# Conditioning chunks of a two-block transformer kernel: from TensorE to VectorE and GpSimd in the first stream

## What is computed

```python
c_act = jax.nn.silu(c)
mod = c_act @ w_ada[l] + b_ada[l]              # (1, 2048) @ (2048, 12288)
sh1, sc1, g1, sh2, sc2, g2 = jnp.split(mod[:, None, :], 6, axis=-1)
```

## Time and profile before

| | |
|---|---|
| median of 3 runs | 3177.53 us (3170.0 to 3181.22) |
| the profiled execution | 3168.41 us, its span 3166.3 us |
| first stream | from the start to about 428 us of the span |
| busy over the span | PE 3005.4 us (95%), PEld 77%, DVE 2092.3 us (66%), ACT 48%, POOL 279.8 us (9%) |
| mean granted clock of TensorE | 0.978 of full speed |
| DMA | 737.98 MB, mean 233 GB/s |

### The profile page before, as it was taken

How to read it: one execution, slowest core, us unless ns; L and a number is a source line. 1 busy time by engine, 2 the same in 40 slices (tenths; PEclk the granted TensorE clock), 3 DMA queues, 4 the chain that set the end, 5 groups by cost and what they waited for, 6 DMA issues and landing times. The chain is left out here.

```text
span 3166.3 us, 43444 instructions
## 1 busy us (share of the span) xinstructions
PE 3005.4 (95%) x17552; PEld 2439.7 (77%) x17552; DVE 2092.3 (66%) x2363; ACT 1510.1 (48%) x1829; POOL 279.8 (9%) x134
## 2 busy tenths in 40 slices
PE   7999978998899999998999999999996999999997
PEld 7888956966776678776788878878785888888886
DVE  5557647365899967766458868745666566666666
ACT  4345522243777755554344475555444444444443
POOL 0000002000000000000000000000003433443330
PEclk9999978999999999998999999999998999999999
DMA  7988567088999978772666744664765566666663
GB/s 263 339 271 298 173 232 290 12 315 306 325 378 348 378 251 271 268 250 82 211 225 218 234 151 158 216 225 160 272 213 186 199 212 213 209 215 212 213 205 125
DMA packets 358136, 737.98 MB, mean 233 GB/s; under 512 B 19957, under 2 KB 118370, under 8 KB 344527
## 3 DMA queue, kind: packets, MB, share of 16 engines
q1 hardware_dynamic: 342740, 710.58, 65.4%
q10 hardware_dynamic: 15228, 25.05, 2.2%
HBM read 708.93 MB, written 26.65 MB: 232 GB/s over the span
## 5 line engine op out<-in xcount | busy, mean ns | idle before, releaser
L288 DVE TENSOR_TENSOR moe_w_lo<-ring,moe_w_hi 128x1024 fp32r<-128x1024 f32 x384 | 458.0, 1222 | 132.7 <-ACT moe_w_hi L278 127.9
L288 DVE TENSOR_TENSOR mx_w_lo<-ring,mx_w_hi 128x1024 fp32r<-128x1024 f32 (+1 forms) x288 | 346.8, 1210 | 279.0 <-ACT mx_w_hi L278 275.3
L278 ACT CAST moe_w_hi<-ring 128x1024 fp32r<-128x1024 f32 x384 | 395.6, 1049 | 247.1 <-PE psum L304 242.6
L278 ACT CAST mx_w_hi<-ring 128x1024 fp32r<-128x1024 f32 (+1 forms) x288 | 296.7, 1036 | 421.2 <-PE psum L304 400.4
L288 DVE TENSOR_TENSOR mlp_w_lo<-ring,mlp_w_hi 128x1024 fp32r<-128x1024 f32 x256 | 318.1, 1244 | 264.5 <-ACT mlp_w_hi L278 263.6
L278 ACT CAST mlp_w_hi<-ring 128x1024 fp32r<-128x1024 f32 x256 | 268.1, 1050 | 407.8 <-PE psum L304 399.1
L304 PE MATMUL psum<-mx_w_hi,mx_a_hi 128*128 128x496 f32 (+1 forms) x1024 | 405.8, 396 | 5.5 <-DVE mx_w_lo L288 4.1
L304 PE MATMUL psum<-mx_w_lo,mx_a_hi 128*128 128x496 f32 (+1 forms) x1024 | 397.7, 388 | 0.0
L304 PE MATMUL psum<-mx_w_hi,mx_a_lo 128*128 128x496 f32 (+1 forms) x1024 | 397.6, 388 | 0.0
L288 DVE TENSOR_TENSOR in_w_lo<-ring,in_w_hi 128x628 fp32r<-128x628 f32 x192 | 155.2, 813 | 167.3 <-ACT in_w_hi L278 165.3
L304 PE MATMUL psum<-in_w_hi,in_a_hi 128*128 128x314 f32 x768 | 242.7, 316 | 2.5 <-DVE in_a_lo L251 1.4
(11 more groups left out here) (615 smaller groups left out, 5728.5 us busy)
## 6 DMA issues: line engine op xcount, KB each, us to landing
ring<-in_w_ada SPq DMA_DIRECT2D x80, 1024.0 KB, 9.2
ring<-in_w_e_gate SPq DMA_DIRECT2D x64, 1024.0 KB, 6.6
ring<-in_w_e_up SPq DMA_DIRECT2D x64, 1024.0 KB, 7.3
ring<-in_w_e_down SPq DMA_DIRECT2D x64, 1024.0 KB, 5.9
ring<-in_w_up SPq DMA_DIRECT2D x64, 1024.0 KB, 5.2
ring<-in_w_down SPq DMA_DIRECT2D x64, 1024.0 KB, 5.1
ring<-in_w_in SPq DMA_DIRECT2D x64, 992.0 KB, 5.1
ring<-in_w_in SPq DMA_DIRECT2D x96, 628.0 KB, 4.7
```

What stands on the lines that cost most here:

```text
L278: self.nc.scalar.copy(self.w[0][:, self._half(j, half), :, 0:cols], self.view[:, slot, ks, 0:cols]).then_inc(self.hi_done, 1)
L288: self.nc.vector.tensor_tensor(self.w[1][:, q, :, 0:cols], self.view[:, j % self.slots, ks, 0:cols], self.w[0][:, q, :, 0:cols].bitcast(F3 ...
```

## The change

The 32 chunks are no longer multiplied on TensorE. A chunk's four column blocks are shared: VectorE takes blocks 0 and 1, GpSimd blocks 2 and 3. Each goes through 64 units (2 parts, 2 blocks, 16 tiles of 128x512, 256 KB) in that order. VectorE does a unit in one instruction (multiply by the column of `c`, add to the total), GpSimd in two, as in the last stage. Units are due every 11/4 ticks, from tick 9 to tick 182; GpSimd isn't bound to ticks and only waits for its data. Each side has three buffers, all in the free part of `ring`, and two totals, in the place of the former buffer. SyncE issues a unit's load once the unit three before it is spent, and due: one tick after that unit's tick for VectorE, three after it for GpSimd. When a group of 16 units is done, TensorE adds its total up over the partitions by one fp32 matmul of ones (32 columns) against 128x512, five ticks after the group's last unit: eight such matmuls in pairs.

```diff
--- before.py
+++ after.py
@@ -542,40 +542,86 @@
 
     SPARE = 32
 
-    def spares(self, st, tiles, conditioned):
-
-        self.tiles, self.conditioned = tiles, conditioned
-        self.filled, self.spent = [st.sem(f"filled{n}") for n in range(2)], st.sem("spent")
-
-    def spare_tick(self, j):
-        return 9 + 15 * j // 4
-
-    def spare_sync(self, sp):
-        for j in range(self.SPARE):
-            yield max(0, self.spare_tick(j - 2) + 1)
-            if j >= 2:
-                sp.wait_ge(self.spent, j - 1)
-            sp.dma_start(self.tiles[j % 2], self.source(0, j)).then_inc(self.filled[j % 2], 16)
+    def spares(self, st, tiles, totals, conditioned):
+
+        self.tiles, self.totals, self.conditioned = tiles, totals, conditioned
+        sems = lambda name: [[st.sem(f"{e}_{name}{n}") for n in range(3)] for e in ("ve", "po")]
+        self.filled = sems("filled")
+        self.spent, self.summed = ([st.sem(f"{e}_{n}") for e in ("ve", "po")] for n in ("spent", "summed"))
+        self.multiplied = st.sem("po_multiplied")
+        self.units = 2 * self.SPARE
+
+    def unit(self, e, u):
+        group, k = divmod(u, KT)
+        part, n = divmod(group, 2)
+        return group, part, 2 * e + n, k
+
+    def spare_tick(self, u):
+        return 9 + 11 * u // 4
+
+    def spare_sync(self, sp, e):
+        w = self.chip.dram["w_ada_2"][0]
+        for u in range(self.units):
+            group, part, b, k = self.unit(e, u)
+            yield max(0, self.spare_tick(u - 3) + 1 + 2 * e)
+            if u >= 3:
+                sp.wait_ge(self.spent[e], u - 2)
+            at = part * D + b * NB
+            sp.dma_start(self.tiles[e][u % 3], w[k * P:(k + 1) * P, at:at + NB]).then_inc(self.filled[e][u % 3], 16)
+
+    def spare_vector(self, ve):
+        nc, at = self.chip.nc, CC["c_2"][0]
+        for u in range(self.units):
+            group, part, b, k = self.unit(0, u)
+            yield self.spare_tick(u)
+            total, c, x = self.totals[0][group % 2], self.chip.cols[:, at + k:at + k + 1], self.tiles[0][u % 3]
+            if u == 0:
+                ve.wait_ge(self.conditioned, 1)
+            if k == 0 and group >= 2:
+                ve.wait_ge(self.summed[0], group - 1)
+            ve.wait_ge(self.filled[0][u % 3], 16 * (u // 3 + 1))
+            if k == 0:
+                ins = nc.vector.tensor_scalar(total, x, c, None, ALU.mult)
+            else:
+                ve.wait_ge(self.spent[0], u)
+                ins = nc.vector.scalar_tensor_tensor(total, x, c, total, ALU.mult, ALU.add)
+            ins.then_inc(self.spent[0], 1)
+
+    def spare_gpsimd(self, po):
+        nc, at = self.chip.nc, CC["c_2"][0]
+        step = Steps(po, self.multiplied)
+        po.wait_ge(self.conditioned, 1)
+        for u in range(self.units):
+            group, part, b, k = self.unit(1, u)
+            total, c, x = self.totals[1][group % 2], self.chip.cols[:, at + k:at + k + 1], self.tiles[1][u % 3]
+            if k == 0 and group >= 2:
+                po.wait_ge(self.summed[1], group - 1)
+            po.wait_ge(self.filled[1][u % 3], 16 * (u // 3 + 1))
+            if k == 0:
+                ins = nc.gpsimd.tensor_scalar(total, x, c, None, ALU.mult)
+            else:
+                step(nc.gpsimd.tensor_scalar(x, x, c, None, ALU.mult))
+                po.wait_ge(self.spent[1], u)
+                ins = nc.gpsimd.tensor_tensor(total, total, x, ALU.add)
+            ins.then_inc(self.spent[1], 1)
 
     def spare_tensor(self, pe):
         nc = self.chip.nc
-        for j in range(self.SPARE):
-            part, k = divmod(j, KT)
-            yield self.spare_tick(j)
-            if j == 0:
-                pe.wait_ge(self.conditioned, 1)
-            if k == 0 and part:
-                pe.wait_ge(self.copied, part)
-            pe.wait_ge(self.filled[j % 2], 16 * (j // 2 + 1))
-            for b in range(4):
-                mm = nc.tensor.matmul(self.bank(part)[32 * b:32 * b + 32], self.c(k), self.tiles[j % 2][:, b],
-                                      start=(k == 0), stop=(k == KT - 1))
-            mm.then_inc(self.spent, 1)
+        for group in range(self.units // KT):
+            yield self.spare_tick(group * KT + KT - 1) + 5
+            for e in range(2):
+                _, part, b, _ = self.unit(e, group * KT)
+                if part and b % 2 == 0:
+                    pe.wait_ge(self.copied, part)
+                pe.wait_ge(self.spent[e], (group + 1) * KT)
+                nc.tensor.matmul(self.bank(part)[32 * b:32 * b + 32], self.chip.c("ones")[:, 0:32],
+                                 self.totals[e][group % 2], start=True, stop=True).then_inc(self.summed[e], 1)
 
     def spare_scalar(self, sc):
         for part in range(self.SPARE // KT):
-            yield self.spare_tick(part * KT + KT - 1) + 1
-            sc.wait_ge(self.spent, part * KT + KT)
+            yield self.spare_tick(part * 2 * KT + 2 * KT - 1) + 7
+            for e in range(2):
+                sc.wait_ge(self.summed[e], 2 * part + 2)
             self.row_out(sc)
 
     def spared(self):
@@ -3466,12 +3512,13 @@
                 engine.wait_ge(stored[q], 16 * ((n + 1 - q) // 2))
 
         da = SparseAttention(chip, st, pool, flat[:, FEW * KC * NB:], qkT, actT, in_dram)
-        ada.spares(st, (st.sb("spare", [P, 4, NB])[:],
-                        flat[:, FEW * KC * W1:FEW * KC * W1 + 4 * NB].rearrange("p (b n) -> p b n", n=NB)), conditioned)
+        free, totals = flat[:, FEW * KC * W1:FEW * KC * NB], st.sb("totals", [P, 4, NB])
+        ada.spares(st, [[free[:, (3 * e + n) * NB:(3 * e + n + 1) * NB] for n in range(3)] for e in range(2)],
+                   [[totals[:, 2 * e + n] for n in range(2)] for e in range(2)], conditioned)
         with nc.Block() as block:
             @block.sync
             def _(sp):
-                tick = Ticks(da.sync(sp), ada.spare_sync(sp))
+                tick = Ticks(da.sync(sp), ada.spare_sync(sp, 0), ada.spare_sync(sp, 1))
                 sp.dma_start(d["proj1"][0:1, DSA_COLS:IN1], qkT[0:1, 0:RW_COLS]).then_inc(zeroed, 16)
                 ring.first(sp, weights, FEW, 3, split.view)
                 for j in range(body):
@@ -3484,7 +3531,8 @@
                 for n in range(FEW):
                     ring.loads[n] += body // FEW - 1
                     split.done(sp, body - FEW + n)
-                sp.wait_ge(ada.spent, ada.SPARE)
+                for e in range(2):
+                    sp.wait_ge(ada.spent[e], ada.units)
                 sp.wait_ge(da.ov_left, len(da.pairs))
                 sp.wait_ge(zeroed, 16)
                 in_dram(sp, blocks)
@@ -3505,6 +3553,10 @@
                                        c == half == 0, c == KC - 1 and half == 1, W1)
                         tick()
                 tick.rest()
+
+            @block.gpsimd
+            def _(po):
+                ada.spare_gpsimd(po)
 
             @block.scalar
             def _(sc):
@@ -3538,7 +3590,7 @@
 
             @block.vector
             def _(ve):
-                tick = Ticks(da.vector(ve))
+                tick = Ticks(da.vector(ve), ada.spare_vector(ve))
                 norm.factors(ve)
                 for q in range(KC):
                     norm.scale(q)
```

## The result

The change makes the kernel slower: 3185.31 us (median of 20 runs) against 3171.95 for the kernel before in the same comparison, a ratio of 1.0038 with a 95% interval of 1.0031 to 1.0045. The ratio leaves out one slow run of 5357.47 us. By the ratio the kernel lost 12 us, by the two medians 13.4, where a gain of 12.4 had been forecast. The profiled execution took 3182.12 us with a span of 3180.2, 13.9 more than the earlier trace rows.

A forecast was written before the change was run, and what follows sets the result against it. The first stream was taken as bound by TensorE; 33.1 us less work, minus 24.7 lost to VectorE, plus 7 of lead, minus 3 for loads, gave 12.4 us gained: 3156.0 us profiled, 3165 against the median, range 3142 to 3191.

The forecast's parts named there:

- the end copy: Last copy of the first stream, starting at 427.50 us of the span before; forecast to come at about 415.
- TensorE's work: First stream: 37.8 us of conditioning matmuls removed, 4.7 us for eight matmuls of ones added, net 33.1 us less.
- VectorE's own units: First stream: 64 units of 0.75 us, 48 us over the stage, 0.27 us per tick, felt where VectorE is full.
- GpSimd's collisions: First stream: one GpSimd unit can hold VectorE for 1.63 us, 0.60 us per tick, times the share f.
- f: Share of GpSimd's possible hold that VectorE feels; bounds 0.21 and 1, taken as 0.6, giving TensorE a 24.7 us loss.
- credit for VectorE's lead: Split weights made ahead absorb some two ticks at the start of three stretches: 0 to 10 us, taken as 7.
- SyncE's waits and late loads: SyncE's queue: late loads and waits for GpSimd's spent count with stream loads behind, put at 3 us (0 to 8).
- full stretches: Index-head rotation, second-half scores, last choosing rounds and q and k rotation, where VectorE was to make TensorE lose 24.7 us.
- The rival of full blocking: First stream with f = 1: loss 38.8 us against 33.1, 5.7 us longer, 3183 us; chance 0.15.
- The rule: A VectorE instruction with two SBUF inputs and a GpSimd instruction reading SBUF exclude each other; the later one fully blocks.
- the four matmuls' price: First stream: each conditioning chunk of four matmuls costs TensorE 1.18 us, 37.8 us for 32 chunks.
- GpSimd wouldn't set the pace: Rival: GpSimd units averaging over 5.8 us lengthen the first stream, at worst by 14 us, 3191 us; chance 0.14.

The follow-up runs named there:

- both narrow, later loads: Changed kernel with VectorE's and GpSimd's unit instructions cut to one column and loads issued three and four ticks after the unit three before: 3144.36 us, ratio 0.9912.
- later loads: Changed kernel with a unit's load issued three (VectorE) and four (GpSimd) ticks after the unit three before, not one and three: 3178.76 us, ratio 1.0023.
- VectorE wide against narrow: With GpSimd at one column, VectorE's units on 512 columns against one: end copy 413.37 against 406.15; with loads issued later, 403.10 against 402.44.
- later loads, GpSimd wide against narrow: Changed kernel with loads issued later, GpSimd's instructions on 512 columns against one: 3178.76 us against 3147.65 us, end copy 435.97 against 403.10.
- without collisions: Changed kernel with GpSimd's instructions cut to one column: 3159.56 us, end copy 413.37; the same with loads issued later: 3147.65 us, end copy 403.10.
- The multiply alone: Changed kernel with GpSimd's addition cut to one column and its multiply whole: 3163.78 us, ratio 0.9970, end copy 421.43.
- later loads and GpSimd narrow: Changed kernel with GpSimd's instructions cut to one column and loads issued three and four ticks after the unit three before: 3147.65 us, ratio 0.9923.
- quiet collisions alone: Changed kernel with loads issued later and GpSimd cut to one column only for units 13 to 20 and 28 to 50: 3150.30 us, ratio 0.9934.
- the uneven version: Against the changed kernel: GpSimd idle in the stage, VectorE does all 128 units, set unevenly, six buffers, later loads: 3152.65 us, ratio 0.9941 to the kernel before.

## Why the prediction was wrong

The forecast's sign was wrong. By its steps, with the end copy as the measure (427.50 before, 440.76 after):

| step of the forecast | put at | measured | from |
|---|---|---|---|
| TensorE's work | -33.1 | -25.1, loads included | both narrow, later loads |
| VectorE's own units | 4.3 | 0.7 with later loads, 7.2 with the change's | VectorE wide against narrow |
| GpSimd's collisions | 20.4 (f = 0.6) | 32.9 | later loads, GpSimd wide against narrow |
| credit for VectorE's lead | -7 | not seen | the same |
| SyncE's waits and late loads | 3 | 4.8 for the order alone, 8.0 with the loads | later loads; first row |
| sum | -12.4 | +13.3 | -25.1 + 0.7 + 32.9 + 4.8 |

The last column adds up by construction, since each step leads from one kernel to the next; another order of steps gives other shares.

**The step that failed** is the size of the collisions, f and the credit together: I put their cost at 20.4 us, set 7 us of lead against it, and so had some 13 us; 32.9 were measured. That is 19.5 of the 25.7 us between -12.4 and +13.3. The other large part is TensorE's work, 8.0 us too high. f was chosen as the middle between a stretch in which VectorE had pauses and the bound of 1. In the full stretches it wasn't near the middle: the forecast's sums give a loss of 42.8 us at f = 1, and 0.45 us less for each 0.01 of f. VectorE's own 4.3 and the 29.9 that the 31 units there cost are 34.2, so f = 0.81, with no lead to set against it and the low clock in it. The trace of before spoke for the higher value, for the multiply of 2.32 us was held for 1.10 of the 1.24 us that GpSimd's addition still ran. That a VectorE with its next instruction always ready meets this each time is my reading of it. The rival of full blocking gave 3183; against the median of before in this comparison, 3171.95, its 5.7 us are 3178, and the result is 6 to 8 us above that.

**The rule** of the Trainium skill, SBUF — State Buffer, "Who interferes with whom", agrees here for GpSimd's additions: one held an instruction of 0.68 us until 1.77. For the multiply the trace does not agree. By the rule the unit that started at 301.35 would have waited until the multiply ended at 302.67; it took 0.23 us longer and ended at 302.33. The multiply alone cost 8.1 us against 22.8 for the addition.

**The second, smaller miss** was where SyncE would wait. The forecast looked at GpSimd's spent count, which is due three ticks late (1.8 us of waits), and not at VectorE's, due one tick after the unit's own tick: 155 us. VectorE's tick comes after ScalarE's and its own work on the half, while SyncE's has only TensorE's use of the chunk ahead of it, so one tick was too little. This closes a loop, from VectorE's unit to SyncE, stream weights, ScalarE and VectorE again; it costs 4.8 us in the changed kernel and 10.3 without collisions (413.37 - 403.10). The last section shows that the 4.8 are mostly low clock.

**What was right:** TensorE bound before; the four matmuls' price, 29.3 us less busy time where 33.1 were summed up; a VectorE unit of 0.75 us (748 ns undisturbed); GpSimd's additions holding VectorE for 1.1 us; that GpSimd wouldn't set the pace (165 us idle for data); and that collisions cost little outside the full stretches (3.0 us). A GpSimd unit took 3.5 us, not the 4 to 5 expected.

## What to carry to other kernels

When work moves from a bound engine to two others, add up what the two do to each other where the busier has no pause, at nearly the full price of a collision (0.81 of it here). The mean busy share hides that. A queue that waits for a consumer belongs behind that consumer's own tick, not its own; and work in small units is best placed unevenly, where the engine has room.

## What the runs showed that I had not expected

TensorE's granted clock fell five times inside the stage of the changed kernel, and never in that of the kernel before. The largest pause ahead of a fall is at tick 63, where TensorE waits for the end of VectorE's rotation (line 3400): 7.1 us in the waits shown above, where the kernel before had 1.0. Windows around it in the changed kernel:

```profile
146.00:153.00 7.00, 0.19 (x2) 0.00 (x0) 6.21 (x11) 2.95 (x5) 4.66 (x3) 0.84 0.52 178
153.00:162.00 9.00, 8.95 (x51) 8.91 (x52) 4.52 (x5) 2.47 (x5) 5.61 (x4) 0.75 0.59 192
```

After 6.8 us idle the clock is at 0.75 on the mean for 9 us, so half of them at the lower level (1.2 GHz), though TensorE is busy throughout. All five stretches at the lower level:

```profile
82.50:85.50 3.00, 3.00 (x13) 3.00 (x13) 2.49 (x3) 2.16 (x4) 2.92 (x3) 0.50 0.91 292
116.50:123.50 7.00, 6.24 (x24) 6.24 (x25) 6.89 (x8) 2.76 (x5) 4.31 (x4) 0.51 0.87 289
150.50:158.00 7.50, 4.95 (x22) 4.91 (x23) 3.67 (x7) 0.60 (x1) 5.42 (x3) 0.54 0.46 156
297.50:301.00 3.50, 3.03 (x13) 2.64 (x12) 3.43 (x4) 1.86 (x3) 2.26 (x2) 0.52 0.66 234
369.00:373.00 4.00, 3.43 (x15) 3.43 (x16) 2.99 (x5) 0.00 (x0) 3.92 (x3) 0.57 0.31 108
```

Each fall came during a pause of TensorE or within 1 us after it; these five pauses lasted 1.9 to 6.8 us. In or ahead of the first, second and fourth, ScalarE had been waiting for late stream weights (8.1, 6.6 and 5.2 us). The 87 matmuls in the five stretches kept TensorE busy for 20.65 us; at the 0.146 us of the prediction they would be 12.7. So an estimate of what the low clock took is 8 us. By the same working it took 3 us in the changed kernel with later loads (two stretches), and nothing in the kernel before, with later loads and GpSimd narrow, with quiet collisions alone, or in the uneven version, whose clock stays at 1.00 from 36 us to the end copy.

The windows from 36 us to the end copy split each cost into TensorE's idle time and its busy time, which holds the low clock. In order: before, changed, later loads, later loads with GpSimd narrow, later loads with both narrow:

```profile
36.00:427.50 391.50, 387.73 (x2683) 347.40 (x2682) 219.35 (x364) 178.66 (x352) 0.00 (x0) 1.00 0.78 261
36.00:440.76 404.76, 371.16 (x2444) 351.76 (x2442) 314.29 (x428) 177.79 (x351) 213.23 (x123) 0.97 0.79 253
36.00:435.97 399.97, 367.57 (x2445) 346.97 (x2443) 317.69 (x428) 179.36 (x351) 213.44 (x124) 0.99 0.80 257
36.00:403.10 367.10, 358.42 (x2444) 342.81 (x2442) 261.19 (x428) 179.14 (x351) 73.38 (x124) 1.00 0.86 280
36.00:402.44 366.44, 358.44 (x2443) 344.31 (x2442) 229.68 (x428) 179.05 (x351) 60.40 (x123) 1.00 0.86 280
```

GpSimd's collisions, from the fourth line to the third, are 23.7 us of idle time and 9.2 of busy time, of which some 3 are the low clock. The order of the loads, from the third to the second, is only 1.2 us of idle time and 3.6 of busy time. So the late loads added little waiting on the whole, and by the two estimates of 8 and 3 us their 4.8 us are for the most part low clock. No run holds the clock fixed, so its share stays an estimate.

Costs also covered each other: later loads bring 4.8 us with collisions and 10.3 without (3.7 when VectorE is narrow too), and GpSimd's two instructions cost 30.9 us one by one and 27.4 together. The falls of the clock may be part of why, since a pause that is moved can take its fall with it; that was not tested.
